# Cumulated decays loaded as rows, decay tiles formed in the scan of the turn before, and the last pair in another order

## The reference, cut to what matters

```python
gc = jnp.cumsum(g.astype(f32).reshape(bn, h, n, c), axis=-1)
decay = jnp.exp(jnp.where(incl, gc[..., :, None] - gc[..., None, :], -jnp.inf))
k_beta = k * beta
m = jnp.where(strict, jnp.einsum('bhnik,bhnjk->bhnij', k_beta, k) * decay, 0.0)
t_inv = lax.linalg.triangular_solve(eye + m, jnp.broadcast_to(eye, m.shape),
                                    left_side=True, lower=True, unit_diagonal=True)
u_val = t_inv @ (v * beta)
w_key = t_inv @ (k_beta * jnp.exp(gc)[..., None])
intra = jnp.einsum('bhnik,bhnjk->bhnij', q, k) * decay
...
def step(s, inp):
    v_new = u_n - w_n @ s
    o_n = qd_n @ s + a_n @ v_new
    s = s * gt_n + jnp.einsum('bhck,bhcv->bhkv', kd_n, v_new)
    return s, o_n
```

## Time and profile before

| | us |
|---|---|
| median of three runs | 846.38 |
| lowest and highest run | 845.85, 852.87 |
| the profiled execution | 845.52 |
| its span | 843.9 |
| PE busy in the span | 754.1 (89%) |
| DVE busy | 578.0 (68%) |
| ACT busy | 418.9 (50%) |
| POOL busy | 202.4 (24%) |

### The profile page before, as it was taken

The page is one execution under the profiler, slowest core; times in us unless marked ns, Lnnn a source line. Parts: engine busy times, 40 slices in busy tenths (PEclk is TensorE's granted clock), DMA queues, the critical chain, the costliest instruction groups (busy, mean ns, idle before and its releaser), DMA issues.

```text
span 843.9 us, 15762 instructions
## 1 busy us (share of the span) xinstructions
PE 754.1 (89%) x6268; PEld 625.6 (74%) x6268; DVE 578.0 (68%) x861; ACT 418.9 (50%) x741; POOL 202.4 (24%) x362
## 2 busy tenths in 40 slices
PE   3998998899979998899669899989999999999974
PEld 1678887889879897799659788887777777687531
DVE  2488587768877688776876448578877775786153
ACT  3476563458434573438524335546565665573101
POOL 3102252203702344013700120011432223212201
PEclk9999999999999999999979999999999999999998
DMA  9966464666527654569866238853999999999992
GB/s 314 298 202 165 112 160 105 189 175 164 144 59 216 182 138 113 148 178 276 263 162 196 62 131 288 333 200 120 333 387 419 407 421 421 416 421 371 419 419 98
DMA packets 164678, 203.10 MB, mean 241 GB/s; under 512 B 33381, under 2 KB 137998, under 8 KB 151674
## 3 DMA queue, kind: packets, MB, share of 16 engines
q1 hardware_dynamic: 162489, 198.02, 69.4%
q0 software_dynamic: 2112, 4.04, 1.3%
HBM read 187.49 MB, written 18.10 MB: 244 GB/s over the span
## 4 chain that ended last, share of the span: by engine, by line
PE 63%; DVE 19%; DMA 10%; issue 3%; ACT 3%; POOL 1%; SPq 1%; POOLq 0%; DVEq 0%; ACTq 0%
PE bank L2558 61%; DMA raw<-in_w_e_dram 5%; DVE chan L1833 3%; DVE half_lo L1737 3%; DVE w_lo L2243 2%; PE bank L2561 2%; DMA raw<-in_w_ada_dram 1%; DMA half_raw<-in_w_out_dram 1%; SPq L622 1%; DVE lane L1913 1%; DVE lane L1942 1%; ACT w_hi L1601 1%; DMA gate_b<-dense 1%; DVE ada_sum L2063 1%; DVE ada_sum L2061 1%
## 5 line engine op out<-in xcount | busy, mean ns | idle before, releaser
L2558 PE MATMUL bank<-hT,half_hi 128*128 128x256 f32 (+1 forms) x1024 | 229.5, 319 | 10.5 <-DVE half_lo L1737 6.3
L2558 PEld LDWEIGHTS bank<-hT,half_hi 128*128 128x128 f32 x1024 | 167.5, 193 | 23.9 <-issue 9.0
L2558 PE MATMUL bank<-hT,half_lo 128*128 128x256 f32 (+1 forms) x512 | 159.9, 312 | 0.0
L1737 DVE TENSOR_TENSOR half_lo<-half_raw,half_hi 128x1024 fp32r<-128x1024 f32 x88 | 108.1, 1230 | 31.4 <-ACT half_hi L1178 30.6
L2243 DVE TENSOR_TENSOR w_lo<-raw,w_hi 128x2048 fp32r<-128x2048 f32 x36 | 88.3, 2462 | 46.5 <-ACT w_hi L1601 46.4
L2558 PE MATMUL bank<-lane 64*64 64x64 f32 (+3 forms) x1968 | 85.4, 229 | 28.3 <-DVE lane L1894 8.2
L1178 ACT CAST half_hi<-half_raw 128x1024 fp32r<-128x1024 f32 x88 | 92.0, 1048 | 32.5 <-DMA half_raw<-in_w_proj_a_dram 12.1
L2558 PEld LDWEIGHTS bank<-lane 64*64 64x64 f32 (+3 forms) x1968 | 76.5, 139 | 38.3 <-issue 21.4
L2558 PEld LDWEIGHTS bank<-hT,half_lo 128*128 128x128 f32 x512 | 98.8, 193 | 5.2
L1601 ACT CAST w_hi<-raw 128x2048 fp32r<-128x2048 f32 x36 | 68.7, 1908 | 34.2 <-PE bank L2558 18.5
L1833 DVE SCALAR_TENSOR_TENSOR chan<-bank,conv_col,chan 128x508 f32<-128x508 f32 (+3 forms) x96 | 63.2, 658 | 10.3 <-ACT chan L1249 7.7
(11 more groups left out here) (392 smaller groups left out, 1385.8 us busy)
## 6 DMA issues: line engine op xcount, KB each, us to landing
raw<-in_w_e_dram SPq DMA_DIRECT2D x96, 1024.0 KB, 10.7
half_raw<-in_w_in_dram SPq DMA_DIRECT2D x64, 512.0 KB, 4.8
half_raw<-in_w_ada_dram SPq DMA_DIRECT2D x32, 512.0 KB, 4.7
raw<-in_w_ada_dram SPq DMA_DIRECT2D x8, 1024.0 KB, 10.9
dense<-staged SPq DMA_DIRECT2D x32, 128.0 KB, 4.6
half_raw<-in_w_proj_a_dram SPq DMA_DIRECT2D x8, 512.0 KB, 5.6
half_raw<-in_w_proj_b_dram SPq DMA_DIRECT2D x8, 512.0 KB, 3.7
half_raw<-in_w_out_dram SPq DMA_DIRECT2D x8, 512.0 KB, 6.8
```

The costliest lines, as they stand in the source:

```text
L1737: dve.tensor_tensor(half_lo[m % HBUF][:, :], half_raw[n % HRING][:, :], half_hi[m % HBUF][:, :].bitcast(F32), ALU.subtract).then_inc(s["ha ...
L2558: return nc.tensor.matmul(dst, lhsT, rhs, start=start, stop=stop)
```

## The change

It has three parts.

**Decays.** The running sums of the log decays are no longer formed by PE in each pair. Two more products at the start give them for all heads as 64 rows of 128 (bank 6, columns 256 to 383), DVE copies these (`cum_rows`), and SP stores them in DRAM (`store_cum`). For each pair SP loads them with `load_cum(p)`: four transfers, each of 512 numbers sent to all 128 partitions (256 KB each), into parts 12 to 15 of `lane`. For the first pair this stands after the first `spill`, for pair `j` in the turn before, in SP's list after `spill(3 + 7 * i + 3)`, and waits until the inverses are placed. `scores(g)` loses its four sums of decays, uses bank `4 + g` for every g, and stands four times in a row at the start of a turn. `decay_exp(p, g)` reads the loaded tiles in SBUF and stands in the scan of the turn before, on ACT. `intra_exp` stays at the turn's start. The tiles move: `p_blk` is now in parts 12, 13, 8 and 9, so `solve_blocks` and `move_inverse` also wait for `intra_exp`. As `scores(3)` is now in bank 7, `turn_out` waits for both query masks of the turn (`intra_ready`) where it waited for the exponentials.

**Order in the scan.** On ACT `new_value(0)` stands ahead of a split instead of behind it, and `ada_line_copy(2 * i + 1)` one `dense_copy` later. On PE `ada_fold(2 * i + 1)` is the last thing of a turn.

**Last pair.** `level_p` stands ahead of `dense(31)` and waits for two groups of the gating sums (`sgu`) instead of four; `level_up`, `quarter_p`, `quarter_up` and `last_p` are spread between `branch_a(0)` to `branch_a(3)` one place earlier. `mix` writes its banks in another order. On DVE `corners` stands after `sgu(1)`, `masks` after `sgu(2)`, and `quarter_copy` and `last_copy` ahead of a `branch_a`. On ACT a split stands ahead of `sgu_high`.

The core of the diff:

```diff
+            def load_cum(p):
+                if p:
+                    sp.wait_ge(s["inverse_placed"], 4 * p)
+                else:
+                    sp.wait_ge(s["landed_cum"], 32)
+                size = 2 * DIRS * P
+                for t in range(TILES):
+                    at_ = (t * PAIRS + p) * size
+                    load(lane_part(12 + t), cum_dram[at_:at_ + size].partition_broadcast(P), s["landed_cum"])
...
                 spill(3 + 7 * i + 3)
+                load_cum(j)
                 after_split(DENSE_AT[3 + 7 * i + 3])
...
+                pool.wait_ge(s["intra_exp"], 2 * i + 2)
                 own.after(pool.memset(solved_blocks, 0.0))
...
-            def decay_exp(g):
-                act.wait_ge(s["scores_ready"], i * 4 + (g + 1))
-                cum = by_pair(bank[6 + g % 2])
+            def decay_exp(p, g):
+                if g == 0:
+                    act.wait_ge(s["landed_cum"], 32 + 64 * (p + 1))
...
-                decay_exp(0)
+                intra_exp(2)
                 ahead(CHAN_AT[j, 0])
-                decay_exp(1)
+                intra_exp(3)
                 center(0)
...
-                decay_exp(2)
-                decay_exp(3)
-                intra_exp(2)
...
+                new_value(0)
                 ahead(DENSE_AT[3 + 7 * i + 3])
-                new_value(0)
...
                 dense_copy(3 + 7 * i + 4)
+                decay_exp(j, 0)
+                decay_exp(j, 1)
                 state_query(2)
                 z_parts(1)
                 new_value(2)
                 ahead(Z_AT[j, 1])
+                decay_exp(j, 2)
                 dense_copy(3 + 7 * i + 5)
+                decay_exp(j, 3)
                 state_query(3)
...
-                    pe.wait_ge(s["intra_exp"], p * 2 + 4)
+                    pe.wait_ge(s["intra_ready"], p * 2 + 4)
...
-                for h in range(2):
-                    for d in range(DIRS):
-                        ins = mm(by_pair(bank[6 + g % 2])[:, h, d, :],
-                                 gates[:, LOG_DECAY, g, 2 * i + h, d:d + 1].to_broadcast([P, P]), causal[:, d, :])
...
             mix()
+            level_p()
             dense(31)
-            level_p()
+            level_up()
             branch_a(0)
-            level_up()
-            branch_a(1)
             quarter_p(0)
             quarter_p(1)
+            branch_a(1)
+            quarter_up()
             branch_a(2)
-            quarter_up()
+            last_p()
             branch_a(3)
-            last_p()
             last_up()
```

110 lines of the change are left out of this document (65 added, 45 removed).

## The result

The changed kernel takes 864.12 us (median of 4 runs, 862.78 to 865.27), the kernel before 848.95 beside it (845.85 to 852.87). The ratio is 1.0166, with a 95% interval of 1.0137 to 1.0195: 1.7% slower. The forecast was 833.5, and the range ended at 843. The profiled execution took 865.27 us.

The account below looks back on a forecast made before the run. PE was taken to bound a turn, with about 8 us of gaps. First turn 5.0 net of the start, two turns 4.8 and last pair 3 made 12.8 off 845.5: 832.7, or 833.5 as median; range 824 to 843.

Parts of the forecast that it names:

- three signs of being wrong: Stall at turn_out under 1 us or over 6, ACT waiting for the rows, or first turn gaining under 3 us.
- the first turn: Without turn_out PE keeps 3.3 us of sums; inverses come about 3.7 sooner; 5.5 us gained with the scan's order.
- The stall at `turn_out`: In turns two and three PE waits about 4.1 us for DVE's second query mask, between 0 and 4.3.
- the sums' gain: PE loses its sums of decays: 3.3 us a pair, given back at turn_out in turns two and three.
- a rival: Little is left: stall costs 1.7 us of clock each, level_p gains nothing, last pair returns its gain; 840.5, chance 0.28.
- the first rival: Masks come in time or the stall is hidden; two turns gain 3.2 us more each; 827, chance 0.15.
- The rows' load: Issued from about 353.5 to 358, landing at 359 to 363, before ACT's 363.8, so the decay tiles cost nothing.
- third rival: Rows land late at decay_exp(j, 0) on ACT; each us past 363.8 costs one in three turns; up to 869, chance 0.07.
- The last pair: level_p 7.5 us sooner, w_proj_a loads 3.8 sooner; gain 3 us, from 1 to 6.
- The scan's order: new_value(0) ahead of the split takes a 0.8 us wait (1.4 in the first turn); ada_fold at the end 0.7.
- The clock: After the new stall half rate could cost up to 1.7 us each time, 3.4 in all; put in the second rival.
- likeliest case: The forecast's own case over the whole kernel: 829 to 838 us, chance 0.5.

Follow-up runs that it names:

- `x5_tiles_later`: Changed kernel with the next pair's decay tiles later in ACT's list of the scan, the first behind new_value(2) and a split: 852.08 us, 1.0042.
- `y1_problems_first`: Changed kernel with decay tiles later and query masks early, plus SP storing the problems ahead of a half's load: 842.89 us, 0.9944.
- `b2s_sums_once`: Kernel before with the sums of decays formed for the first pair only (output not the reference's): 850.69 us against 850.94, 0.9997.
- `x6_both`: Changed kernel with decay tiles later on ACT and both query masks right behind the first taps on DVE: 842.53 us, 0.9919.
- `y2_last_back`: Changed kernel with decay tiles later and masks early, plus the old order of PE, DVE and ACT in the last pair: 841.11 us, 0.9915.
- `z4_fill_out`: Changed kernel with decay tiles later, plus 17 unread products filling PE's stall ahead of turn_out: 852.05 us, 1.0025.
- `z2_fill_level`: Changed kernel with tiles later, masks early in turns two and three, plus ten unread products ahead of level_p in the three turns: 843.19 us, 0.9916.
- `z3_mix_sooner`: Changed kernel with tiles later, masks early in turns two and three, plus mix_raw loaded ahead of an ada line's last store: 839.85 us, 0.9886.
- `x1_rows_early`: Changed kernel with the four loads of the next pair's rows moved between the second and third ada half on SP: 873.64 us, 1.0288.
- `y4_no_rows`: Changed kernel with tiles later and masks early, without the row loads for pairs 1 to 3 (output not the reference's): 841.27 us, 0.9916.

## Why the prediction was wrong

Two of the forecast's three signs of being wrong came: ACT waited for the rows, and the first turn gained under 3 us.

**The stall at `turn_out`: right, its price too small.** 4.1 us were forecast for the second and third turn, at the mask's end 21.0 us after `scores(0)`; 4.3 and 4.5 were measured, at 21.0 and 21.2. That it returned the sums' gain was right too, and POOL did start sooner, by 3.9 and 2.2 us where some 4 were forecast. What the stall draws behind it was left to a rival: 2.0 us of lower clock, and SP standing with PE, so that POOL's blocks, done 35.4 and 34.7 us after `scores(0)`, were stored only at 40.5 and 39.3 (the third turn's at 38.6 before, about 38 forecast). `level_p` came 2.1 and 1.2 us later than before, not 0.9 sooner. Between the forecast and the first rival the stall was priced at 6.4 us; taking it away brought 9.5, so some 3 us of the miss are here.

**The rows' load: the step that failed.** I took 5.4 us to land, issued "from about 353.5 to 358" and wanted at 363.8. So the wait was put at nothing ("they cost nothing if their rows have landed by 363.8"). The time to land was the smaller error: 6.4 us each on the page, and 10.5 from the first issue to the last landing, where my numbers make 9.9. The larger one was the issue itself. I counted it from where the inverses are placed, not from where SP's list lets it stand: behind a bias and the `spill` of `dense_copy(3 + 7 * i + 3)`, at 73.4 us after `scores(0)` and not 68.7. That is 4.7 us, the length of ACT's wait (4.56). My own third rival had the place right, "`decay_exp(j, 0)` on ACT, ahead of `state_query(2)`", and the price, each us a us in three turns; what it lacked was a look at the queue, and so it got 0.07. Asking for them too early cost 12.0 us (`x5_tiles_later`), which was none in the sum: this is the step that made the kernel slower.

**The first turn: the second step that failed.** 5.5 us were forecast, and even with the tiles later the profiled first turn is as long as before, 95.6 us. PE kept its 3.3 us, and lost most of them ahead of `level_p`: the gap there grew from 1.1 to 3.9 us, `level_p` came 0.8 us sooner and `quarter_p` 0.7 later. "The problems are ready some 4 us sooner now, so POOL ends sooner" skipped SP again. DVE had the problems 6.8 us after `scores(0)`, but SP's stores stood behind the load of a half, went out at 10.3 instead of 13.3, and landed 8.6 us later instead of 5.1. POOL started at 22.9, before at 22.2. Where they do go first (`y1_problems_first`), POOL starts at 16.5 in the first turn, and the blocks stored at 37.0 are loaded only at 42.9: the queue takes the gain on the way back.

**The value of PE's work.** "PE keeps its 3.3 us" treated a us of PE as a us of the turn. `b2s_sums_once` took 9.9 us of it away from the kernel before, and nothing that the runs can tell came of it. It left the sums of the first pair in place, so it does not measure the 3.5 us of the first turn; there the gaps above do. My reading of the 3.1 us gap, that such a us counts only if the problems' way gets shorter, was borne out: in the second and third turn, where that way got shorter (`x6_both`), the turns gained 5.1 us each. The sum gave the first turn its 3.5 us without asking SP's list for it.

**The last pair.** 3 us were forecast, from 1 to 6, and `y2_last_back` shows none. The term was the weights' loads, 3.8 us sooner; the load of `gate_a` with its tanh, which PE's wait at 472.29 follows, was in none of the sums. Nor was the load of `mix_raw`, for which PE waits 4.5 us there. In the first 40 us of the last pair the DMA engines are busy 0.89 of the time. The changed kernel's first solved step is 0.8 us later than before.

**The scan's order.** The 0.8 us of `new_value(0)` and the 1.2 of `ada_fold` are gone from PE's waits as forecast, about 5 us of the sum; in their place stands a wait of 0.7 us a turn for `new_value(3)`. Alone in the kernel before the moves bring 2.7 us (0.1 to 0.5%).

**The clock.** Named, with a row and a rule, and left out of the likeliest case. The 2.0 us at `turn_out` are close to the 1.7 of the rival. By the Trainium skill, "TensorE: Matmul & The Clock Gate", Part 1, the clock halves after idle time; by that rule, the trace agrees (0.50 behind the empty stall, 1.00 behind the filled one). But keeping it up saved nothing of the time that the runs can tell (`z4_fill_out` has 0.9983 of the ratio without the products, `z2_fill_level` 1.0006).

**The sum again, by profiled executions.** Against the forecast's span of 831.1 us the changed kernel has 32.5 more: 11.5 in the first turn, 8.8 and 7.5 in the two others, 4.5 behind them and 0.3 ahead. With both edits (`x6_both`) 7.2 remain: 6.2 in the first turn, 5.7 behind the turns and 0.8 ahead of them, and 2.7 less than forecast in each of the two others. By the runs, the 30.6 us between the forecast and the measured time are 12.0 of the rows, 3.1 of the stall beyond its price, and 15.5 that no edit removed. That last part lies in the first turn and behind the turns. SP's order in the first turn and the waits of the last pair are seen in the profiles, but where an edit took one of them away (`y1_problems_first`, `z3_mix_sooner`) the next one stood there, so the cause of this part stays open.

## What to carry to other kernels

Before a us of work is taken from the busiest engine, look whether its gaps end with something that travels (a store, another engine, a load): if so the work can be worth nothing until that way is shorter: 9.9 us were worth under 1.8 here. Place a load by where its issuing queue really stands, which is behind every wait in its list, and put the instruction that needs it as late as its user allows: moving that instruction saved 12 us, moving the load cost 9.5. A us gained by one engine in front of a shared queue can be lost to the transfer just ahead of it: POOL's 3 us in `y1_problems_first` were.

## What the runs showed of the hardware

- A transfer of 1 MB in four loads, each 512 numbers sent to all 128 partitions, issued ahead of a 512 KB half made that half land after 10.0 us, where the page's medians are 4.7 and 5.1 (`x1_rows_early`); with nothing wanted behind it, it cost nothing that the runs can tell (`y4_no_rows` 0.9916 without, `x6_both` 0.9919 with).
- Small stores right behind a half landed after 8.6 us in the first turn of the changed kernel (issue to the next issue that waits for them) instead of 5.1 before. The two small stores of the solved blocks took 5.8 us with a half issued 0.4 us ahead of them (`y1_problems_first`, third turn) and 2.4 with one 3.5 us ahead (`x6_both`).
- With 4 us of idle array the granted clock stood at 0.50 for the next 4 us of full work (`x5_tiles_later`); with products that nobody reads in the idle time it stood at 1.00 (`z4_fill_out`). The profiled busy time of PE moved by 11.6 us (756.3 to 744.7) at the same 6144 records between the changed kernel and `x6_both`.
